# The last layer norm of an encoder trunk: variance about a half row's mean, squares in halves, output in three parts

## Reference

```python
x = layer_norm(ALPHA * x + 0.5 * swiglu(x, ffn2_w13[l], ffn2_w2[l]), ln_g[l, 3], ln_b[l, 3])

def layer_norm(x, g, b):
    mu = jnp.mean(xf, axis=-1, keepdims=True)
    var = jnp.mean(jnp.square(xf - mu), axis=-1, keepdims=True)
    y = (xf - mu) * lax.rsqrt(var + LN_EPS) * g + b
```

## Time and profile before

| | us |
|---|---|
| median of 3 runs | 1084.83 |
| lowest, highest | 1084.27, 1085.13 |
| span of the profiled execution | 1083.1 |
| TensorE busy | 1073.4 (99%) |
| VectorE busy | 867.7 (80%) |
| ScalarE busy | 535.0 (49%) |
| GpSimd busy | 83.9 (8%) |

### The profile page before, as it was taken

How to read it: one execution, slowest core, us unless ns; L and a number is a source line. 1 busy time by engine, 2 the same in 40 slices (tenths; PEclk the granted TensorE clock), 3 DMA queues, 4 the chain that set the end, 5 groups by cost and what they waited for, 6 DMA issues and landing times.

```text
span 1083.1 us, 16448 instructions
## 1 busy us (share of the span) xinstructions
PE 1073.4 (99%) x5582; PEld 924.3 (85%) x5582; DVE 867.7 (80%) x1496; ACT 535.0 (49%) x735; POOL 83.9 (8%) x141
## 2 busy tenths in 40 slices
PE   9999999999999999999999999999999999999997
PEld 7888888999998888888888888889999988888885
DVE  6988877887855898878688887878978668987885
ACT  6544444666544644444455444445665545444442
POOL 0015001230000000000000000001300000000000
PEclk9999999999999999999999999999999999999999
DMA  9976675455564487665557666654544654866641
GB/s 320 294 224 189 215 221 149 136 176 170 162 223 154 137 257 212 193 202 186 163 181 249 202 192 194 196 159 132 175 155 159 222 169 134 267 193 202 183 146 40
DMA packets 156467, 203.98 MB, mean 188 GB/s; under 512 B 12960, under 2 KB 136096, under 8 KB 156416
## 3 DMA queue, kind: packets, MB, share of 16 engines
q1 hardware_dynamic: 152112, 192.55, 56.4%
q0 software_dynamic: 3488, 9.97, 3.3%
q10 hardware_dynamic: 816, 0.79, 0.2%
HBM read 202.22 MB, written 1.05 MB: 188 GB/s over the span
## 4 chain that ended last, share of the span: by engine, by line
PE 98%; DMA 0%; DVE 0%; issue 0%; POOL 0%; DVEq 0%; ACT 0%; POOLq 0%; ACTq 0%
PE ps L615 96%; PE ps L698 1%; DMA raw<-in_ffn_w 0%; PE ps L1101 0%; PE ps L869 0%; PE ps L956 0%; PE ps L1009 0%; DVE x L1609 0%; PE ps L1061 0%; DVE x L1585 0%; PE ps L993 0%; PE ps L1062 0%; PE ps L1063 0%; DVE tmp L1596 0%; POOL x L1891 0%
## 5 line engine op out<-in xcount | busy, mean ns | idle before, releaser
L1461 DVE TENSOR_TENSOR w_lo<-raw,w_hi 128x1024 fp32r<-128x1024 f32 (+3 forms) x246 | 297.4, 1221 | 47.8 <-ACT w_hi L1195 45.5
L1195 ACT CAST w_hi<-raw 128x1024 fp32r<-128x1024 f32 (+3 forms) x246 | 252.9, 1044 | 161.4 <-PE ps L615 149.0
L615 PE MATMUL ps<-w_hi,xT 128*128 128x512 f32 (+1 forms) x912 | 286.8, 389 | 0.8 <-ACT w_hi L1187 0.8
L615 PEld LDWEIGHTS ps<-w_hi,xT 128*128 128x128 f32 x912 | 170.9, 188 | 37.0 <-issue 1.9
L1523 DVE STREAM_TRANSPOSE hidden_T<-ev 32x128 f32<-32x128 f32 x624 | 189.0, 303 | 11.2
L615 PE MATMUL ps<-w_hi,mixT 128*128 128x512 f32 x688 | 197.5, 390 | 0.0
L615 PE MATMUL ps<-v_flat,xT 128*128 128x512 f32 (+1 forms) x660 | 177.0, 389 | 0.0
L615 PE MATMUL ps<-w_lo,xT 128*128 128x512 f32 (+1 forms) x456 | 175.2, 388 | 0.0
L1195 ACT CAST v_flat<-raw 128x1024 fp32r<-128x1024 f32 (+1 forms) x114 | 118.2, 1045 | 85.3 <-PE ps L615 83.4
L615 PEld LDWEIGHTS ps<-w_hi,mixT 128*128 128x128 f32 x688 | 128.6, 188 | 26.3
L615 PEld LDWEIGHTS ps<-v_flat,xT 128*128 128x128 f32 x660 | 123.8, 188 | 25.3 <-DVE cqp L1461 0.2
(11 more groups left out here) (177 smaller groups left out, 1250.1 us busy)
## 6 DMA issues: line engine op xcount, KB each, us to landing
raw<-in_ffn_w SPq DMA_DIRECT2D x350, 256.0 KB, 3.6
raw<-in_ffn_w SPq DMA_DIRECT2D x88, 512.0 KB, 4.3
raw<-in_mem_wkv SPq DMA_DIRECT2D x32, 512.0 KB, 4.5
raw<-in_w_out SPq DMA_DIRECT2D x16, 512.0 KB, 4.5
raw<-in_mem_wq SPq DMA_DIRECT2D x16, 512.0 KB, 4.2
raw<-in_mem_wo SPq DMA_DIRECT2D x16, 512.0 KB, 6.4
gb<-in_ln_g POOLq DMA_DIRECT2D x16, 256.0 KB, 5.5
gb<-in_ln_b POOLq DMA_DIRECT2D x16, 256.0 KB, 5.3
```

The costliest lines, as they stand in the source:

```text
L615: return nc.tensor.matmul(dst, stand, move, start=start, stop=stop, skip_group_check=True)
L1195: nc.scalar.copy(slot_hi[slot[n]][:, 0:size], raw[:, n % RAW, 0:size]).then_inc(hi_done, 1)
L1461: nc.vector.tensor_tensor(slot_lo[slot[n]][:, s], raw[:, n % RAW, s], slot_hi[slot[n]][:, s].bitcast(F32), ALU.subtract).then_inc(lo_done, 1)
```

## The change

The four stores become five. SyncE stores block 0's two halves, block 1's upper half (columns 512 to 1023) and the first quarter of block 1's row; ScalarE stores the second quarter. For block 1:

- VectorE makes twice the first half's sum over D, negative, before block 0's shift: the negative mean of the first half row. ScalarE squares each half row about this mean, as two operations, the second after the second residual.
- After the second residual VectorE makes the mean, the distance of the two means, its square less epsilon, centers the upper half, and takes the two sums of squares in with one operation each: the variance is the mean square about the first half's mean less the square of the distance.
- VectorE centers the lower half behind the variance. It waits for this and for GpSimd's power, then shifts the upper half and the second quarter.
- ScalarE scales the first quarter, GpSimd adds its bias, and SyncE stores it.

```diff
@@ -417,6 +417,7 @@
         x_columns_landed = [sem(f"x_columns_landed{j}") for j in range(KT // 2)]
         x_hi, x_lo, mem_hi, mem_lo = sem("x_hi"), sem("x_lo"), sem("mem_hi"), sem("mem_lo")
         last_scaled = sem("last_scaled")
+        last_sums, last_centered, last_shifted, last_added = sem("last_sums"), sem("last_centered"), sem("last_shifted"), sem("last_added")
         row_gains_landed, pscale_landed = sem("row_gains_landed"), sem("pscale_landed")
         dve_step, pool_step = sem("dve_step"), sem("pool_step")
         angles_ready, tables_done = sem("angles_ready"), sem("tables_done")
@@ -474,6 +475,7 @@
         VEPS = [st[:, 30 + 4 * b:31 + 4 * b] for b in range(2)]
         RSTD = [st[:, 31 + 4 * b:32 + 4 * b] for b in range(2)]
         SUMSQ = [st[:, 84 + 2 * b:86 + 2 * b] for b in range(2)]
+        NEG_FIRST, NEG_APART, APART_SQ, SQ_FIRST, SQ_SECOND = (st[:, k:k + 1] for k in range(16, 21))
         MS, RMS = ([st[:, q + 2 * b:q + 2 + 2 * b] for b in range(2)] for q in (88, 92))
         MX, NEGM, SUM, REC = ([st[:, 36 + 12 * q + 4 * i:40 + 12 * q + 4 * i] for i in range(3)] for q in range(4))
 
@@ -588,12 +590,15 @@
                     n = u + 10 + LOOP_UNITS * LOOPS
             for n in range(n, UNITS):
                 load(n, source[n][1])
-            for b in range(TB):
-                for c in range(HALVES):
-                    cols = slice(c * D // 2, (c + 1) * D // 2)
-                    sp.wait_ge(norm_done, normed(4 * L - 1, b, c))
-                    sp.dma_start(out[0, b * P:(b + 1) * P, cols], x[:, b, cols]).then_inc(stored, 16)
-            sp.wait_ge(stored, 16 * TB * HALVES)
+            for c in range(HALVES):
+                cols = slice(c * D // 2, (c + 1) * D // 2)
+                sp.wait_ge(norm_done, normed(4 * L - 1, 0, c))
+                sp.dma_start(out[0, 0:P, cols], x[:, 0, cols]).then_inc(stored, 16)
+            sp.wait_ge(last_shifted, 1)
+            sp.dma_start(out[0, P:2 * P, D // 2:D], x[:, 1, D // 2:D]).then_inc(stored, 16)
+            sp.wait_ge(last_added, 1)
+            sp.dma_start(out[0, P:2 * P, 0:D // 4], x[:, 1, 0:D // 4]).then_inc(stored, 16)
+            sp.wait_ge(stored, 16 * 5)
 
         def landed(n):
 
@@ -1301,7 +1306,17 @@
                 if place is None:
                     act.wait_ge(rstd_ready, 2 * e + 1)
                     nc.scalar.mul(centered[0][:, D // 2:D], centered[0][:, D // 2:D], RSTD[0]).then_inc(last_scaled, 1)
-                    squares(e, 1)
+                    act.wait_ge(mean_ready, 2 * e + 2)
+                    nc.scalar.activation(bank(0), x[:, 1, 0:D // 2], ACT.Square, bias=NEG_FIRST, scale=1.0,
+                                         accum_out=SQ_FIRST).then_inc(squares_summed, 1)
+                    act.wait_ge(last_sums, 1)
+                    nc.scalar.activation(bank(1), x[:, 1, D // 2:D], ACT.Square, bias=NEG_FIRST, scale=1.0,
+                                         accum_out=SQ_SECOND).then_inc(squares_summed, 1)
+                    act.wait_ge(rstd_ready, 2 * e + 2)
+                    act.wait_ge(last_centered, 1)
+                    nc.scalar.mul(centered[1][:, 0:D // 4], centered[1][:, 0:D // 4], RSTD[1]).then_inc(last_scaled, 1)
+                    act.wait_ge(last_shifted, 2)
+                    act.dma_start(out[0, P:2 * P, D // 4:D // 2], x[:, 1, D // 4:D // 2]).then_inc(stored, 16)
                     return
                 ahead_to(plan.units_by[done["y", e, 1] - 1] + 2)
                 if FILL[l, place]:
@@ -1442,6 +1457,7 @@
 
                 steps[0] += 1
                 ins.then_inc(dve_step, 1)
+                return ins
 
             def settle(it=None):
                 dve.wait_ge(dve_step, plus(steps[0], it, STEPS))
@@ -1582,7 +1598,7 @@
 
                     dve.wait_ge(pe_done, done[tag])
                     z = x[:, b, c * 512:(c + 1) * 512]
-                    own(nc.vector.scalar_tensor_tensor(out=z, in0=ps[:, 4 + 2 * b + c, :], scalar=weight, in1=z,
+                    return own(nc.vector.scalar_tensor_tensor(out=z, in0=ps[:, 4 + 2 * b + c, :], scalar=weight, in1=z,
                                                        op0=ALU.mult, op1=ALU.add, accum_out=ROWSUM[b][c]))
 
                 def mean(b):
@@ -1624,14 +1640,38 @@
                     settle()
                 variance(0)
                 residual(1, 0, ("half y", e))
+                def center_half(c):
+
+                    cols = slice(c * D // 2, (c + 1) * D // 2)
+                    return nc.vector.scalar_tensor_tensor(out=centered[1][:, cols], in0=x[:, 1, cols], scalar=NEGMEAN[1],
+                                                          in1=gb[:, 0, cols], op0=ALU.add, op1=ALU.mult)
+
                 if place is None:
+                    settle()
+                    nc.vector.tensor_scalar(NEG_FIRST, ROWSUM[1][0], -2.0 / D, None, ALU.mult).then_inc(mean_ready, 1)
                     shift(0, [0])
-                    residual(1, 1, ("y", e, 1))
-                    mean(1)
-                    center(1)
-                    variance(1)
-                    dve.wait_ge(norm_done, normed(e, 0, 1))
-                    shift(1)
+                    dve.wait_ge(pe_done, done["y", e, 1])
+                    z = x[:, 1, D // 2:D]
+                    nc.vector.scalar_tensor_tensor(out=z, in0=ps[:, 7, :], scalar=weight, in1=z, op0=ALU.mult, op1=ALU.add,
+                                                   accum_out=ROWSUM[1][1]).then_inc(last_sums, 1)
+                    dve.wait_ge(last_sums, 1)
+                    own(nc.vector.tensor_scalar(NEGMEAN[1], ROWSUM[1][0], ROWSUM[1][1], -1.0 / D, ALU.add, ALU.mult))
+                    own(nc.vector.tensor_scalar(NEG_APART, ROWSUM[1][0], ROWSUM[1][1], 1.0 / D, ALU.subtract, ALU.mult))
+                    settle()
+                    own(nc.vector.tensor_scalar(APART_SQ, NEG_APART, NEG_APART, LN_EPS / ALPHA ** 2, ALU.mult, ALU.subtract))
+                    own(center_half(1))
+                    settle()
+                    dve.wait_ge(squares_summed, 2 * e + 3)
+                    own(nc.vector.tensor_scalar(SQ_FIRST, SQ_FIRST, 1.0 / D, APART_SQ, ALU.mult, ALU.subtract))
+                    settle()
+                    nc.vector.tensor_scalar(VEPS[1], SQ_SECOND, 1.0 / D, SQ_FIRST, ALU.mult, ALU.add).then_inc(var_ready, 1)
+                    center_half(0).then_inc(last_centered, 1)
+                    dve.wait_ge(last_centered, 1)
+                    dve.wait_ge(rstd_ready, 2 * e + 2)
+                    for cols in (slice(D // 2, D), slice(D // 4, D // 2)):
+                        nc.vector.scalar_tensor_tensor(out=x[:, 1, cols], in0=centered[1][:, cols], scalar=RSTD[1],
+                                                       in1=gb[:, 1, cols], op0=ALU.mult, op1=ALU.add)\
+                            .then_inc(last_shifted, 1)
                     return
                 first, fills = first_of_stage(e), plan.units_by[done["y", e, 1] - 1]
                 if e % 4 in (0, 3):
@@ -1890,6 +1930,10 @@
                         pool.wait_ge(norm_done, normed(e, 0, 0))
                         nc.gpsimd.tensor_tensor(x[:, 0, D // 2:D], centered[0][:, D // 2:D], gb[:, 1, D // 2:D], ALU.add)\
                             .then_inc(norm_done, 1)
+                    if e == 4 * L - 1 and b == 1:
+                        pool.wait_ge(last_scaled, 2)
+                        nc.gpsimd.tensor_tensor(x[:, 1, 0:D // 4], centered[1][:, 0:D // 4], gb[:, 1, 0:D // 4], ALU.add)\
+                            .then_inc(last_added, 1)
                 if e < 4 * L - 1 and e % 4:
                     pool.wait_ge(norm_done, normed(e, 1, 1))
                     load_gains(e + 1)
```

## The result

The changed kernel takes 1086.80 us (median of 12 runs, 1086.38 to 1088.09) against 1084.72 us (12 runs of the kernel before beside it): a ratio of 1.0017 with a 95% interval of 1.0010 to 1.0024. So it is slower by about 2.1 us, or 0.17%. That is little, but it is clear of noise: the interval leaves out 1, and the fastest run of the changed kernel (1086.38) is above the slowest of the kernel before (1085.38). The forecast was 1086.6 us.

A forecast was written before the change was run, and what follows sets the result against it. After TensorE's last product a serial tail runs, and GpSimd's closing DRAIN was taken to end the program. Its last operation ending later outweighed the stores' +0.5: +1.8 on 1084.83 gave 1086.6 us, range 1084.9 to 1087.2.

The forecast's parts named there:

- What bounds the kernel: TensorE to its last product, then block 1's serial tail; GpSimd's 5.086 us DRAIN ends last, 0.7 us after SyncE's.
- Residual and sums: Last norm: the first half's mean (0.15 us) and squares are hidden; the second half's squares end 0.65 us earlier on ScalarE.
- VectorE's new chain: Last norm's variance: 0.75 us of centering and three small operations eat ScalarE's 0.65; ready at 77.80, not 77.74: +0.06.
- The power beside centering: GpSimd's last power is held up by VectorE's lower-half centering and ends at 78.86 instead of 78.36: +0.50 us.
- The three parts: Block 1's output: GpSimd's add ends at 80.23, VectorE's quarter, slowed by 0.40 us, at 80.56.
- The stores: Last stores: landing 1.68 to 2.03 us after issue, the last at 82.28 to 82.63 against 81.98: +0.3 to +0.65, taken +0.5.
- The end: GpSimd's closing DRAIN follows its later last operation: +1.68 counted from its start, +1.87 from its end; taken +1.8 us.
- Rival (a): Program end: the DRAIN is no cost of its own but ends with the stores; +0.3 to +0.65, 1085.3 us; chance 0.24.
- Rival (b): Output tail: GpSimd's add waits for both VectorE shifts and ends at 80.63; +2.27, 1087.1 us; chance 0.17.
- Rival (c): Tail: the DRAIN is free and VectorE and GpSimd nowhere hold each other up; -0.5, 1084.3 us; chance 0.06.
- Rival (d): Last norm: ScalarE's squares still on the path, needing halves of over 1.2 us each; no chance given.

The follow-up runs named there:

- extra DRAIN: Kernel before plus one GpSimd DRAIN ahead of the last norm: 1084.62 us (ratio 0.9996), repeated 1084.19 (0.9993); the same edit on the changed kernel: 1085.07 (1.0000).
- late operation: Kernel before plus a one-column GpSimd power into an unused place, issued after VectorE's last shift: 1087.37 us, ratio 1.0022.
- count of DMAs: Kernel before with 54 more small GpSimd DMAs (108): 1210.7 us, one execution; kernel before with gains and biases as whole rows (38 DMAs): 1084.51 us, ratio 0.9994.
- without the add: Changed kernel without ScalarE's and GpSimd's quarter; VectorE shifts the whole lower half, SyncE stores it as one: 1085.65 us, ratio 1.0005 against the kernel before.
- centering last: Changed kernel with the lower half's centering issued only after GpSimd's power is done: 1087.17 us, one run.
- variance first: Changed kernel with the upper half's centering moved behind the variance: 1086.62 us, one run.
- three parts: Kernel before plus a GpSimd DRAIN ahead of the last norm and only the change's three-part output, with whole-row squares and centering: 1084.43 us, one run.

## Why the prediction was right

The forecast lay 0.2 us from the median, and the interval's 1.1 to 2.6 us hold its +1.8. By the medians the change costs 2.08 us, by the two traces 1.94. The prediction counted its 0.17% as no change; with 12 runs of each kernel it is measured as slower. Its main step, the DRAIN, had stood on two rows and a chance of 0.52 when it was written; the experiments, and not the number, bear it out. Its steps:

- **What bounds the kernel.** Right. The DRAIN as a cost of its own was a reading of two rows; the extra DRAIN, the late operation and the count of DMAs show it. The Trainium skill's page "VectorE: DVE Perf Modes", section "The DRAIN you can't avoid", has such DRAINs at about 12 ns on every engine; the 5.35 us here differ from it, and the measurement decides. Of the two ways to count it, 4.50 from the last operation's end was right and 5.09 from its start wrong: the DRAIN's duration was 5.09, 5.35, 5.52, 5.26 and 5.26 us in five kernels with 54 DMAs (before, changed, without the add, centering last, variance first), and the distance from the operation's end 4.50 in all of them. Only with the late operation, which the program waits for, was it 4.66.
- **Residual and sums.** Hidden, as said; a half row's squares took 0.67 and 0.69 us for a price of 0.72.
- **VectorE's new chain.** +0.06 forecast, +0.06 measured (+2.41 to +2.47).
- **The power beside centering.** +0.50 forecast and measured (+3.04 to +3.54). The Trainium skill's page "SBUF — State Buffer", section "SBUF: two separate sides", with its lock of the pair of ports, agrees: 0.99 us beside the centering, 0.55 without it.
- **The three parts.** GpSimd's add was to end 4.90 us after the residual's start and ended at 4.97; after VectorE's upper shift it took 0.58, not 0.47. VectorE's quarter was to end at 5.23 and ended at 5.26. The prediction said that the earlier trace rows don't part the 0.59 us lost by the two operations, and chose 0.40 for the second. Narrower windows of the same trace do part them (the rows below): the second took 1.63 us for a mean of 1.23, so 0.40 was right there, and the add ended 0.46 us after the first. In the changed kernel the second's loss comes to 0.47 (0.95 us for a quarter of 0.48).
- **The stores.** +0.3 to +0.65, taken at +0.5; measured 7.20 - 6.65 = +0.55. The 128 KB stores land 1.82 us (SyncE) and 1.91 us (ScalarE) after their issue, between the bounds of 1.68 and 2.03.
- **The end.** +1.68 or +1.87; measured +1.94, the second of the two plus the 0.07 of the add.

The two operations of the earlier trace rows one by one, in narrower windows of the trace of before:

```profile
215.62 1.42 DVE L1461 TENSOR_TENSOR w_lo<-raw,w_hi 128x1024 fp32r<-128x1024 f32 x1
...
216.96 1.63 DVE L1461 TENSOR_TENSOR w_lo<-raw,w_hi 128x1024 fp32r<-128x1024 f32 x1
```

Rival (a) is refuted by the late operation. Rival (b) is refuted by the profile: the add ends at 1080.69, inside VectorE's last shift, which ends at 1080.97. Rival (c) fell with both of its conditions. Rival (d), the squares still on the path, did not come either: their sum was there at +1.55, 0.43 us before the centering that VectorE waited for had ended.

## What to carry to other kernels

Look at what ends last behind the last useful operation, engine by engine, before moving work to an idle engine: here the idlest one had the latest end, since every DMA that it had issued cost 0.082 us behind its last operation. Give such an engine a DRAIN of its own in an earlier gap, or issue fewer and larger DMAs from it; either was worth 0.70 us by the trace. The medians of these two kernels over several runs, 1084.2 to 1084.6 us, lie 0.5 to 0.7 us below the kernel before's, but their intervals hold 1, so the gain is read from the traces. And two engines that exclude each other don't share work: a quarter handed to GpSimd made VectorE later.

## What the runs showed of the hardware

GpSimd's DRAIN costs 0.082 us for each DMA that GpSimd issued since the last one, whatever its size (38, 54 and 108 DMAs: 3.20, 4.50, 8.91 us behind the last operation), and nothing once an earlier DRAIN has paid for them (0.07 us). A DRAIN's row says little by its duration, since it begins 0.04 us before the last operation's row, or behind it where the program waits for that operation: what repeats is the distance between the two ends. The hold-up between VectorE and GpSimd goes both ways. GpSimd's power took 0.99 us beside a centering and 0.55 without one. And GpSimd's add, issued during the first of two back-to-back shifts, ends 0.58 to 0.62 us after that one, and the second takes 0.95 to 0.98 us for 0.48 (changed kernel, centering last, variance first, three parts).
